# Another start-up order for a fused four-layer network kernel: X fetched by ACT, its squares summed on POOL

## The reference

```python
def rmsnorm(x, w):
    xf = x.astype(jnp.float32)
    y = xf * lax.rsqrt(jnp.mean(xf * xf, axis=-1, keepdims=True) + EPS)
    return (y * w.astype(jnp.float32)).astype(x.dtype)
...
x = x + lru_mlstm_layer(rmsnorm(x, e_norm[j]), e_w_in[j], ...)
...
    u = x @ w_in
    x_l, x_m, z = jnp.split(u, [LRU_WIDTH, LRU_WIDTH + MLSTM_WIDTH], axis=-1)
    x_mc = jax.nn.silu(causal_conv(x_m, conv_m_w, conv_m_b))
```

## Time and profile before

| | |
|---|---|
| three executions | 3475.84, 3478.89, 3481.37 us |
| median | 3478.89 us |
| the profiled execution's own time | 3480.91 us |
| its span, first to last instruction | 3479.0 us (1.9 us lie around it) |
| granted TensorE clock, mean of the span | 0.998 of full speed |
| PE busy / DVE busy / ACT busy / POOL busy | 98% / 79% / 55% / 50% |
| DMA, mean of the span | 179 GB/s |

### The profile page before, as it was taken

How to read it: one execution, slowest core, us unless ns; L and a number is a source line. 1 busy time by engine, 2 the same in 40 slices (tenths; PEclk the granted TensorE clock), 3 DMA queues, 4 the chain that set the end, 5 groups by cost and what they waited for, 6 DMA issues and landing times.

```text
span 3479.0 us, 52970 instructions
## 1 busy us (share of the span) xinstructions
PE 3414.5 (98%) x19584; PEld 2967.4 (85%) x19584; DVE 2733.3 (79%) x3931; ACT 1896.5 (55%) x2906; POOL 1726.3 (50%) x1473
## 2 busy tenths in 40 slices
PE   8999999999999999999999999999999999999999
PEld 7888788888888888888888888888888888888888
DVE  8769887679999976787888758877688888658875
ACT  6555785455565554775544434444765544444443
POOL 4325772168888832143566306653143666306640
PEclk9999999999999999999999999999999999999999
DMA  5554555655555556544555665566544555665566
GB/s 188 171 166 158 168 182 182 186 196 173 186 175 170 186 165 187 191 140 134 189 192 189 188 193 189 190 185 194 189 139 141 188 189 192 187 191 192 189 187 182
DMA packets 177041, 624.38 MB, mean 179 GB/s; under 512 B 19784, under 2 KB 25616, under 8 KB 175760
## 3 DMA queue, kind: packets, MB, share of 16 engines
q1 hardware_dynamic: 171216, 606.11, 55.3%
q10 hardware_dynamic: 5568, 14.89, 1.2%
HBM read 618.75 MB, written 2.17 MB: 178 GB/s over the span
## 4 chain that ended last, share of the span: by engine, by line
PE 79%; DVE 10%; issue 4%; ACT 3%; POOL 3%; DMA 0%; ACTq 0%; SPq 0%; POOLq 0%; DVEq 0%
PE psG L531 50%; PE psG L532 25%; DVE WL L1281 3%; ACT WH L773 1%; DVE Et L1574 1%; ACT L793 1%; PE psM L555 1%; DVE sdx L1294 1%; POOL SQ L1763 1%; POOL GV L1913 1%; DVE sds L1323 0%; DVE sdx L1586 0%; DVE sds L1310 0%; PE psM L516 0%; DVE Y L1286 0%
## 5 line engine op out<-in xcount | busy, mean ns | idle before, releaser
L531 PE MATMUL psG<-H,WH 128*128 128x512 f32 x6032 | 2148.9, 400 | 16.1 <-DVE H L1288 12.3
L1281 DVE TENSOR_TENSOR WL<-RAW,WH 128x1024 fp32r<-128x1024 f32 (+1 forms) x1162 | 1524.1, 1312 | 481.9 <-ACT WH L773 479.2
L773 ACT ACTIVATE WH<-RAW 128x1024 fp32r<-128x1024 f32 (+1 forms) x1162 | 1214.2, 1045 | 865.7 <-PE psG L532 841.3
L532 PE MATMUL psG<-H,WL 128*128 128x256 f32 x6032 | 1685.0, 279 | 0.0
L531 PEld LDWEIGHTS psG<-H,WH 128*128 128x128 f32 x6032 | 1133.9, 188 | 279.4 <-issue 17.2
L532 PEld LDWEIGHTS psG<-H,WL 128*128 128x128 f32 x6032 | 1141.0, 189 | 3.1
L531 PE MATMUL psG<-Y,WH 128*128 128x512 f32 x2944 | 1035.7, 397 | 1.0 <-DVE Y L1286 1.0
L532 PE MATMUL psG<-Y,WL 128*128 128x256 f32 x2944 | 823.0, 280 | 0.0
L531 PEld LDWEIGHTS psG<-Y,WH 128*128 128x128 f32 x2944 | 552.7, 188 | 130.4 <-DVE Y L1286 1.3
L532 PEld LDWEIGHTS psG<-Y,WL 128*128 128x128 f32 x2944 | 556.5, 189 | 0.5
L1922 POOL TENSOR_SCALAR fou<-fsu,PAR 128x256 f32<-128x256 f32 x88 | 179.2, 2037 | 550.6 <-DVE fsu L1323 550.6
(11 more groups left out here) (354 smaller groups left out, 3362.0 us busy)
## 6 DMA issues: line engine op xcount, KB each, us to landing
RAW<-in_w_up SPq DMA_DIRECT2D x352, 512.0 KB, 3.7
RAW<-in_w_o_in SPq DMA_DIRECT2D x162, 512.0 KB, 3.7
RAW<-in_w_e_in SPq DMA_DIRECT2D x128, 512.0 KB, 3.6
RAW<-in_w_down SPq DMA_DIRECT2D x128, 512.0 KB, 3.5
RAW<-in_w_in SPq DMA_DIRECT2D x112, 512.0 KB, 3.6
RAW<-in_w_o SPq DMA_DIRECT2D x72, 512.0 KB, 3.6
RAW<-in_w_e_out SPq DMA_DIRECT2D x64, 512.0 KB, 3.8
RAW<-in_w_o_out SPq DMA_DIRECT2D x64, 512.0 KB, 3.7
```

Source lines behind the costliest of these rows:

```text
L531: e.matmul(o, wh, x, start=k == 0, stop=False, skip_group_check=True)
L532: ins = e.matmul(o[:, 0:T], wl, x[:, 0:T], start=False, stop=last, skip_group_check=True)
L773: copy = lambda o, i, scale=1.0: e.activation(o, i, ACT.Copy, scale=scale)
L1281: tt(WL_[c % NRAW][:, 0:n], RAW_[c % NRAW][:, 0:n], WH_[c % NW][:, 0:n].bitcast(F32), SUB).then_inc(sem("wl"), 1)
```

## The change

Five things, all in `start()` of the engines and in `first_norm`.

1. ACT issues the constants `KC`, the first 16 columns of `pa` (`e_norm`) and the four parts of X. SP starts with the chunks 0, 1, 2, then the rest of `pa`, then chunk 3. The semaphore `kc` now counts both small transfers (32).
2. ACT makes the highs of a part first and then the high half of a chunk; it waits for the rest of `pa` only after all of them.
3. DVE does, for each part, the four lows, then the low half of the chunk, then the three squares.
4. POOL, after its four squares, adds the 15 other squares into `fn[3]`, one after another. PE multiplies the ones by this one tile ahead of beat 8 (`colsum`), and ACT makes `rstd` at b == 8 in place of 7.
5. PE begins with 20 products of the ones by themselves into a PSUM bank that nobody reads.

```diff
@@ PE
         def first_norm(b):
-            for i in range(3 * (b - 1), min(3 * b, 16)) if 1 <= b <= 6 else ():
-                if i % 4 == 3:
-                    w.wait_ge(sem("fn_sqp"), i // 4 + 1)
-                else:
-                    w.wait_ge(sem("fn_sqd"), i // 4 * 3 + i % 4 + 1)
-                sums("fn", i, fn[i], 16)
+            if b == 8:
+                w.wait_ge(sem("fn_sqp"), 1)
+                colsum("fn", fn[3])
...
+        w.wait_ge(sem("ones"), 1)
+        for _ in range(20):
+            e.matmul(psM[3][:, 0:P], ones, ones, start=True, stop=True)
         for b in range(NB):
@@ ACT
         def start():
-            split_hi(0)
-            w.wait_ge(sem("pa"), 16)
+            e.dma_start(KC[:, :], I["c_cols"]).then_inc(sem("kc"), 16)
+            e.dma_start(PAR[0][:, 0:16], I["pa"][:, 0:16]).then_inc(sem("kc"), 16)
+            for i in range(4):
+                e.dma_start(X_[:, i * 1024:(i + 1) * 1024], I["xT"][:, i * 1024:(i + 1) * 1024]).then_inc(sem(f"x{i}"), 16)
+            w.wait_ge(sem("kc"), 32)
             for i in range(16):
                 w.wait_ge(sem(f"x{i // 4}"), 16)
                 high(0, i, par("pa", "e_norm", i))
-                if i in (3, 7):
-                    split_hi(i // 4 + 1)
+                if i % 4 == 3 and i < 12:
+                    split_hi(i // 4)
+            w.wait_ge(sem("pa"), 16)
...
         def first_norm(b):
-            if b == 7:
+            if b == 8:
                 root(small["fn"], rstd, 1.0 / D, sem("rstd"))
@@ DVE
             e.memset(ones, 1.0).then_inc(sem("ones"), 1)
-            split_lo(0)
-            w.wait_ge(sem("pa"), 16)
+            w.wait_ge(sem("kc"), 32)
             for part in range(4):
                 w.wait_ge(sem(f"x{part}"), 16)
-                for i in range(4 * part, 4 * part + 3):
-                    tt(fn[i], X[i], X[i], MUL).then_inc(sem("fn_sqd"), 1)
                 for i in range(4 * part, 4 * part + 4):
                     w.wait_ge(sem("hh"), i + 1)
                     low(HL[i], X[i], HH[i], par("pa", "e_norm", i), sem("hl"))
-                if part < 2:
-                    split_lo(part + 1)
+                if part < 3:
+                    split_lo(part)
+                for i in range(4 * part, 4 * part + 3):
+                    tt(fn[i], X[i], X[i], MUL).then_inc(sem("fn_sqd"), 1)
+            w.wait_ge(sem("pa"), 16)
@@ POOL
         def start():
             for part in range(4):
                 w.wait_ge(sem(f"x{part}"), 16)
-                tt(fn[4 * part + 3], X[4 * part + 3], X[4 * part + 3], MUL).then_inc(sem("fn_sqp"), 1)
+                own.up(tt(fn[4 * part + 3], X[4 * part + 3], X[4 * part + 3], MUL))
+            for i in range(16):
+                if i == 3:
+                    continue
+                w.wait_ge(own.sem, own.n)
+                if i % 4 < 3:
+                    w.wait_ge(sem("fn_sqd"), i // 4 * 3 + i % 4 + 1)
+                ins = tt(fn[3], fn[3], fn[i], ADD)
+                if i < 15:
+                    own.up(ins)
+            ins.then_inc(sem("fn_sqp"), 1)
@@ SP
-        x_part(0)
-        e.dma_start(KC[:, :], I["c_cols"]).then_inc(sem("kc"), 16)
-        e.dma_start(PAR[0][:, 0:columns("pa")[1]], I["pa"]).then_inc(sem("pa"), 16)
         fetch(0)
-        x_part(1)
         fetch(1)
         fetch(2)
-        x_part(2)
-        x_part(3)
+        e.dma_start(PAR[0][:, 16:columns("pa")[1]], I["pa"][:, 16:]).then_inc(sem("pa"), 16)
         fetch(3)
```

More of the change, by code:

```diff
@@ L787, in root @@
             w.wait_ge(sem("small"), use.done)
-            w.wait_ge(sem("kc"), 16)
+            w.wait_ge(sem("kc"), 32)
             for s, v in rl_read:
@@ L1948, in fetch @@
             e.dma_start(RAW_[c % NRAW][:, 0:n], src[:, col:col + n]).then_inc(sem(f"raw{c % NRAW}"), 16)
-        def x_part(i):
-            e.dma_start(X_[:, i * 1024:(i + 1) * 1024], I["xT"][:, i * 1024:(i + 1) * 1024]).then_inc(sem(f"x{i}"), 16)
-        x_part(0)
-        e.dma_start(KC[:, :], I["c_cols"]).then_inc(sem("kc"), 16)
-        e.dma_start(PAR[0][:, 0:columns("pa")[1]], I["pa"]).then_inc(sem("pa"), 16)
         fetch(0)
-        x_part(1)
         fetch(1)
         fetch(2)
-        x_part(2)
-        x_part(3)
+        e.dma_start(PAR[0][:, 16:columns("pa")[1]], I["pa"][:, 16:]).then_inc(sem("pa"), 16)
         fetch(3)
```

## The result

The changed kernel takes 3492.92 us (median of 5 runs, 3486.63 to 3494.94), beside 3477.61 for the kernel before in the same session (3473.99 to 3481.37, 5 runs). The ratio is 1.0041, with an interval of 1.0029 to 1.0052. The profiled execution took 3494.71, its span is 3492.9 at a mean clock of 0.994 (before 3479.0 at 0.998). The forecast was 3482.7 in a range of 3475 to 3490: too fast by 10 us.

What follows compares the result with a forecast made beforehand. Bound: DVE's first multiplication by `rstd`, which PE follows at 72.53. POOL's sum at 35.4 plus 2.9 gives 38.3 against 34.49, +3.8 us; on the three-run median 3478.9 that makes 3482.7 us, range 3475 to 3490.

Steps and rivals of the forecast that it cites:

- The clock that counts: DVE's first multiplication of xm 0 by `rstd`, at 34.49 before; each us later there makes PE later at 72.53.
- X part 0 at 7.3: Landing of X's first part, with ACT's and SP's transfers taking equal shares: 7.3 us, bounds 5.7 and 9.5.
- PE's start at 12.5: PE's first block after X part 0, table load, highs and chunk 0's halves: 12.5 us, 0.2 later than before.
- 20 ones cost nothing and give nothing: PE's starting products end by 10 us, before 12.5, at no cost; 2 us saved in beats 0 and 1 is waited away.
- 15 ones gone are turned into waiting before beat 8: Products of ones taken off PE save 6.9 us, all of which PE spends waiting before beat 8.
- The sum done at 35.4: POOL's 15 additions start at 17.4 and take 1.2 us each, 18 us in all.
- DVE's chain "ends at 30.6 plus what POOL takes from it": DVE's chain to the low half of chunk 5 (28.35 before) starts at 11.4 and ends at 30.6 plus POOL's unpriced share.
- From the sum to the multiplication 2.9: PE's product 0.6, ACT's Ln, table load and Exp 2.2, handing over 0.1: multiplication at 38.3, +3.8 us.
- the sum is in time: Rival: POOL adds at 0.87, sum done at 29, ACT's order decides; multiplication -2 to -0.5, 3477 us; 15%.
- The clock's drop: If the clock drops in PE's wait before beat 8, half-speed beats cost about 2.5 us, just fitting PE's slack.
- The slower rival: POOL's additions meet DVE's long pieces nearly every time; at pitch 1.68 the sum ends at 42.6, +11.0, 3490 us; 17%.

Runs made afterwards that it cites:

- a_x_first: The changed kernel with ACT issuing X part 0 ahead of the two small transfers: 3487.93 us, ratio 1.0026 to the kernel before.
- a_x_sp: The changed kernel with SP issuing X, `KC` and `pa` as before: 3487.7 us, ratio 1.0031 to the kernel before.
- a_no_ones: The changed kernel without its 20 products of ones: 3489.89 us, ratio 1.0034 to the kernel before.
- a_warm: The changed kernel with 56 products of ones in place of 20, up to the first operand: 3490.18 us, ratio 1.0038 to the kernel before.
- a_pool_late: The changed kernel with POOL's additions held back until DVE is through with chunk 5: 3492.36 us, ratio 1.0042 to the kernel before.
- b_ones: The kernel before with 26 products of ones that nobody reads at PE's start: 3477.09 us, ratio 0.9996.
- b_warm: The kernel before with 43 products of ones that nobody reads at PE's start: 3477.9 us, ratio 1.0001.
- b_r_warm: The kernel before with fp32r squares, ones in groups of four, ACT's root one beat sooner and 44 starting products of ones: 3476.4 us, ratio 0.9998.
- a_fill: The changed kernel with 28 more products of ones ahead of beat 6: 3489.2 us, ratio 1.0032 to the kernel before.
- a_fill_22: The changed kernel with 22 more products of ones ahead of beat 6: 3485.55 us, ratio 1.0032 to the kernel before.
- b_pool_sum: The kernel before with only the sum of squares moved to POOL: 3485.43 us, ratio 1.0021.

## Why the prediction was wrong, step by step

- **The clock that counts** (when DVE can multiply xm 0 by `rstd`; "each us that this comes later, PE gets later at 72.53"). Right; it is the line of the table, to 0.1 us.
- **X part 0 at 7.3.** Wrong: 10.4. Equal shares between the two queues was right in packets and wrong in bytes. The sum counted the two small transfers as two issues of 0.45 us; their 256 packets were not counted at all, though the change lists them ahead of X. At the multiplication X's delay is worth 3.3 us (a_x_first) or 3.1 (a_x_sp) within the change.
- **PE's start at 12.5.** 15.71, with the 3.1 from X. The terms behind it were right: table load 1.28, highs 1.6, high half of chunk 0, low half 1.2.
- **20 ones cost nothing and give nothing.** Right, and that was measured two ways (a_no_ones, a_warm). They ended at 7.7, not 10.
- **15 ones gone are turned into waiting before beat 8.** Right in kind. The wait came ahead of beat 6 instead.
- **The sum done at 35.4.** 35.70. The right number by luck, out of wrong terms: the additions began as forecast (17.30, 17.4), at a pitch of 0.88 and not 1.2, and waited 5.7 us for DVE's squares, which I had not counted.
- **DVE's chain "ends at 30.6 plus what POOL takes from it".** This is the step that failed. It was left without a number, and then the sum went on as if it were zero: "beat 8 starts at about 35.9". I had the row for it, four lows at 2.37 in place of 1.66 beside POOL's squares, 0.7 us in one group of four. I put the whole price of the two engines' exclusion on POOL's side, as a pitch of 1.2. The runs show it on DVE's: 7.0 us up to the low half of chunk 3. The rule that I weighed from the Trainium skill ("SBUF — State Buffer", "SBUF: two separate sides"), that the two engines exclude each other for whole instructions, fits the rows in kind: lows at 0.94 beside additions of 0.79, in turns. It does not fit in full: one low and one addition together take 0.88 us there, and alone they follow at 0.40 and 0.80, which is 1.20. What I drew from it, that POOL waits, is half of it. DVE waits too, and here nearly all of the waiting was DVE's.
- **From the sum to the multiplication 2.9.** 10.25. It assumed PE at beat 8 when the sum is ready. PE's product stands in PE's order behind beat 7, and PE was still waiting for chunk 3 (36.84), so the sum lay idle for 6.4 us (35.70 to 42.12). Then came ACT's half and high half 7 ahead of Ln, which I had named in the rival "the sum is in time" and not in the forecast.
- **The clock's drop, "about 2.5 us, fits just into" PE's slack.** The size was right to a tenth (2.54), the place and the beats wrong. It was on the path, since beats 6 and 7 stand between chunk 3 and xm 0.
- **The slower rival** (17%) had the right total, 11.0 us at the multiplication, from the wrong mechanism: additions at 1.68, a sum done at 42.6. The additions were never slow.

The 11.46 us then are: X late and the table load behind it with the new order, 5.3 at DVE's first low half (14.43, 9.12) and 3.4 of it left at chunk 3 (28.06 less 24.61, from a_pool_late); POOL's additions 7.0; together 10.42, and 0.5 for the stretched low half itself, of which 6.52 reach beat 6, as it had stood 4.5 behind that low half before (25.8, 30.32); the half clock 2.5; and 2.4 as the remainder, which ACT's order and the product behind beat 7 account for in the timelines and no run took apart. The 0.7 us more at beat 36 is the clock again: behind the wait of 2.45 us at 83.89 it stood at half, and the first pairs of beat 35 take 0.64.

```profile
84.00:86.00 2.00, 2.00 (x7) 1.72 (x8) 2.00 (x5) 1.67 (x4) 1.91 (x1) 0.50 0.00 0
```

What is left open is 1.8 us behind beat 100, which is inside the scatter of the table's third column.

## What to carry to other kernels

When work is moved to a second engine that excludes the first from a shared resource, price it on both: what the moved instruction takes itself, and what each instruction of the engine beside it then takes; the second may be the path. Follow a moved result through the order of every engine that handles it: a sum that is ready waits for whatever stands ahead of its reader. And count a transfer's packets, not only its bytes, when it stands ahead of a large one on a queue that shares its engines with another.

## What was not expected of the hardware

- DVE's lows took 0.94 us beside additions on POOL and 0.47 alone, squares in groups of three 1.63 in place of 1.08, while an addition took 0.79 in place of 0.72. Nearly all of the exclusion was paid by one side. Each such addition had begun just ahead of DVE's instruction (17.30 and 17.42 for the first). Where DVE had begun first, with a low half, POOL paid: 1.77 us for an addition in a_pool_late. Who begins first fits these rows; no run varied it. It was so with the sum on POOL in the kernel before too (four lows 3.60 in place of 1.66).
- Two small transfers ahead of X, 256 packets of 32 and 64 bytes, kept 0.5 MB back by 3.8 us (10.45, 6.66), of which 0.9 is the later issue; in the same time the other queue moved as many packets of 4 KB.
- ACT's table load, which ran at 0.72 us before, sat behind the wait for X at 10.46 once the first activation had that wait.
- The granted clock of a window is noted as 1.00 where PE ran nothing before it, as in the earlier trace rows and without the 20 products (12 to 18 us), while the pairs of blocks there take 0.64 as at half clock; with products ahead the same blocks are noted at 0.50. There the durations tell the clock, and the column does not. The changed kernel without its 20 products, 12 to 18 us:

```profile
12.00:18.00 6.00, 1.98 (x6) 1.69 (x7) 5.28 (x8) 5.99 (x14) 3.45 (x4) 1.00 1.04 401
```

- Products of ones that end 3.4 us ahead of the first block left it at half clock (b_ones); ones that ended 0.15 or less ahead left it at full (a_warm, b_warm), and so did a gap of 0.74 (b_r_warm). After a standstill of 6.4 us beats 6 and 7 ran at half clock; after products that filled it, at full. After waits of 2.45 to 2.63 us beat 35 ran at half clock in four executions (the changed kernel, a_x_first, a_fill, a_warm), and after a wait of 2.44 at full in four others (a_no_ones, a_fill_22, b_pool_sum, a_x_sp). The nearest of these waits are 0.01 us apart, and no run shows what decided.
